# First attention of a two-block transformer kernel: row maxima come out negated, keys carry the factor of an eighth

## The reference, cut to what matters

```
# 8 MoBA heads (one block of 256 keys here, so: causal attention with a bias by distance)
s = q @ k.T * (1 / sqrt(64)) + bias[h, bucket(dist)];  s = where(dist >= 0, s, -inf)
p = softmax(s);  o = p @ v
# 8 sliding-window (SWA) query heads over 2 key heads, window 128, with one learned sink each
s = q @ k.T * (1 / sqrt(64)) + bias[h, bucket(dist)];  s = where(allowed, s, -inf)
m = max(max(s), sink)
p = exp(s - m) / (sum(exp(s - m)) + exp(sink - m));  o = p @ v
# 4 memory heads of width 128 over 256 memory rows
p = softmax(q @ km.T / sqrt(128));  o = p @ vm
```

## Time and profile before

| | |
|---|---|
| median of three runs | 2535.05 us |
| lowest, highest | 2534.59, 2536.48 us |
| span of the profiled execution | 2532.4 us |
| median less span | 2.65 us |
| instructions in the span | 40162 |
| TensorE matmul busy | 2480.0 us, 98% |
| VectorE busy | 1435.8 us, 57% |
| ScalarE busy | 1080.1 us, 43% |
| GpSimd busy | 1313.3 us, 52% |
| first attention, from its first scores to the last unit's output | about 122 to 176 us of the span |

### The profile page before, as it was taken

The page is one execution under the profiler, slowest core; times in us unless marked ns, Lnnn a source line. Parts: engine busy times, 40 slices in busy tenths (PEclk is TensorE's granted clock), DMA queues, the critical chain, the costliest instruction groups (busy, mean ns, idle before and its releaser), DMA issues.

```text
span 2532.4 us, 40162 instructions
## 1 busy us (share of the span) xinstructions
PE 2480.0 (98%) x13612; PEld 2128.2 (84%) x13612; DVE 1435.8 (57%) x3281; ACT 1080.1 (43%) x2021; POOL 1313.3 (52%) x661
## 2 busy tenths in 40 slices
PE   9899999999999999999999999999999999999999
PEld 9789999898888888777888888888888888789888
DVE  5476666379883513565666556665554464755431
ACT  5375555542323332466353222342222343575554
POOL 5628877844434443333434443444443454456887
PEclk9999999999999999999999999999999999999999
DMA  7728545655555432121334444544443453234564
GB/s 243 231 76 256 186 150 185 180 166 189 187 162 146 139 100 76 59 67 51 116 100 145 139 148 135 166 131 149 149 144 110 132 174 123 92 101 150 181 193 141
DMA packets 407170, 365.15 MB, mean 144 GB/s; under 512 B 7564, under 2 KB 398302, under 8 KB 407056
## 3 DMA queue, kind: packets, MB, share of 16 engines
q1 hardware_dynamic: 384840, 339.21, 42.6%
q10 hardware_dynamic: 22216, 24.43, 2.9%
HBM read 362.53 MB, written 1.08 MB: 144 GB/s over the span
## 4 chain that ended last, share of the span: by engine, by line
PE 86%; DVE 5%; POOL 3%; issue 3%; ACT 1%; DMA 1%; SPq 0%; DVEq 0%; POOLq 0%; ACTq 0%
PE bank L2251 67%; PE bank L2261 5%; POOL w_lo L874 3%; PE bank L2259 3%; PE bank L2895 2%; PE bank L2935 1%; PE bank L2349 1%; PE bank L2350 1%; PE bank L2356 1%; ACT w_hi L941 1%; DVE stat L2155 1%; PE bank L2921 1%; PE bank L2497 1%; PE bank L2498 0%; PE bank L2502 0%
## 5 line engine op out<-in xcount | busy, mean ns | idle before, releaser
L874 POOL TENSOR_TENSOR w_lo<-raw,w_hi 128x1024 fp32r<-128x1024 f32 (+3 forms) x557 | 1211.6, 2188 | 1067.3 <-ACT w_hi L941 1067.0
L2251 PE MATMUL bank<-u_both,w_hi 128*128 128x512 f32 (+1 forms) x4240 | 1093.8, 348 | 13.0 <-POOL w_lo L874 6.8
L941 ACT ACTIVATE w_hi<-raw 128x1024 fp32r<-128x1024 f32 (+3 forms) x558 | 534.2, 974 | 1019.7 <-PE bank L2251 817.2
L2251 PEld LDWEIGHTS bank<-u_both,w_hi 128*128 128x128 f32 x4240 | 741.5, 190 | 123.9 <-issue 14.9
L2251 PE MATMUL bank<-u_both,w_lo 128*128 128x512 f32 (+1 forms) x2120 | 734.5, 346 | 0.0
L2251 PEld LDWEIGHTS bank<-u_both,w_lo 128*128 128x128 f32 x2120 | 403.5, 190 | 49.2
L1717 DVE SCALAR_TENSOR_TENSOR bank<-mod_raw,cond,bank 128x256 f32<-128x256 f32 x1008 | 401.2, 482 | 0.4 <-DMA mod_raw<-in_w_mod 0.4
L2251 PE MATMUL bank<-hid_hi,w_hi 128*128 128x512 f32 x528 | 205.7, 390 | 0.0
L2251 PE MATMUL bank<-hid_hi,w_lo 128*128 128x512 f32 x528 | 205.4, 389 | 0.0
L2251 PE MATMUL bank<-hid_lo,w_hi 128*128 128x512 f32 x528 | 205.4, 389 | 0.0
L2039 DVE TENSOR_TENSOR bank<-bank,work 128x512 f32<-128x512 f32 (+1 forms) x88 | 55.5, 630 | 193.8 <-PE bank L2251 186.8
(11 more groups left out here) (327 smaller groups left out, 3617.2 us busy)
## 6 DMA issues: line engine op xcount, KB each, us to landing
mod_raw<-in_w_mod SPq DMA_DIRECT2D x144, 512.0 KB, 4.7
raw<-in_ffn_w_in SPq DMA_DIRECT2D x69, 1024.0 KB, 5.1
raw<-in_w_in SPq DMA_DIRECT2D x67, 1024.0 KB, 5.2
raw<-in_ffn_w_out SPq DMA_DIRECT2D x56, 704.0 KB, 4.7
raw<-in_w_ffn_up SPq DMA_DIRECT2D x22, 1024.0 KB, 5.0
raw<-in_ffn_w_in ACTq DMA_DIRECT2D x19, 1024.0 KB, 5.3
raw<-in_w_attn_out SPq DMA_DIRECT2D x8, 1024.0 KB, 5.1
raw<-in_w_o SPq DMA_DIRECT2D x8, 1024.0 KB, 5.1
```

The lines of the kernel that those rows point to most:

```text
L874: pool.tensor_tensor(st.half(t, w_lo[slot]), st.half(t, block), st.half(t, w_hi[slot]).bitcast(f32), ALU.subtract).then_inc(lo_ready, 1)
L941: act.activation(st.half(t, w_hi[(st.first + c) % 2]), st.half(t, raw_of(st, n)), ACT.Copy).then_inc(hi_ready, 1)
L2251: ins = pe.matmul(dst, s, v, start=first and n == 0, stop=final and n == 2)
```

## The change

Keys of the MoBA and SWA heads are multiplied by 0.125 when they are copied out of PSUM (the copy takes a scale), the bias tables are no longer multiplied by 8, and the exponential's scale is 1 for those units. The reduces for the maxima write negated results (`negate=True`). A MoBA unit then needs no further step: its second reduce raises `nmax_ready`. An SWA unit takes the minimum with the negated sink (a new tile `minus_sinks`, 64 bytes in each partition, filled by one new VectorE instruction). A memory unit still multiplies, now by plus the scale. The two reduces of a MoBA or SWA unit are no longer linked to each other. Behind `minus_sinks` every tile lies 64 bytes further on in SBUF.

```diff
         sinks = sb("sinks", [P, 8])
+        minus_sinks = sb("minus_sinks", [P, 16])
...
-            def copy_tiles(dst, cols):
+            def copy_tiles(dst, cols, scale=1.0):
...
-                                       .rearrange("p (o t) -> p o t", o=1), ACT.Copy).then_inc(taken[b], 1)
+                                       .rearrange("p (o t) -> p o t", o=1), ACT.Copy, scale=scale).then_inc(taken[b], 1)
...
-            gemm("qk_mb", copy_tiles(qk_mb, slice(0, S)))
+            moba_queries, moba_keys = copy_tiles(qk_mb, slice(0, S)), copy_tiles(qk_mb, slice(0, S), 0.125)
+            gemm("qk_mb", lambda st, i, c: (moba_queries, moba_keys)[i](st, i, c))
...
-                        ins = act.activation(k_sw[64 * to:64 * to + 64, kv, :], bank[0][64 * kv:64 * kv + 64, 0:S], ACT.Copy)
+                        ins = act.activation(k_sw[64 * to:64 * to + 64, kv, :], bank[0][64 * kv:64 * kv + 64, 0:S], ACT.Copy, scale=0.125)
...
-                scale = 0.125 if kind != "mem" else 1.0 / math.sqrt(128)
+                scale = 1.0 if kind != "mem" else 1.0 / math.sqrt(128)
...
+            dve.tensor_scalar(minus_sinks[:, 0:8], bank[4][:, 0:8], -1.0, None, ALU.mult)
             dve.tensor_copy(sinks[:, :], bank[4][:, 0:8]).then_inc(taken[4], 1)
...
-                dve.tensor_scalar(tables[:, v, :], bank[5 - v][0:8, :], 8.0, None, ALU.mult).then_inc(taken[5 - v], 1)
+                dve.tensor_copy(tables[:, v, :], bank[5 - v][0:8, :]).then_inc(taken[5 - v], 1)
...
             def max1(n):
                 kind, h = UNITS1[n]
-                scale = 0.125 if kind != "mem" else 1.0 / math.sqrt(128)
                 dve.wait_ge(score_ready, n + 1)
                 st_ = stat[:, n % 2, :]
+                minus = st_[:, 2:4] if kind == "moba" else st_[:, 0:2]
                 if causal(n):
-                    for q in range(2):
-                        link(dve.tensor_reduce(st_[:, q:q + 1], bank[SCORE1[n % 4]][:, q * S:q * S + keys1(n, q)], AX.X, ALU.max))
+                    ins = [dve.tensor_reduce(minus[:, q:q + 1], bank[SCORE1[n % 4]][:, q * S:q * S + keys1(n, q)], AX.X, ALU.max,
+                                             negate=True) for q in range(2)][-1]
                 else:
-                    link(dve.tensor_reduce(st_[:, 0:2], bank[SCORE1[n % 4]][:, :].rearrange("p (q k) -> p q k", q=2), AX.X, ALU.max))
+                    ins = dve.tensor_reduce(minus, bank[SCORE1[n % 4]][:, :].rearrange("p (q k) -> p q k", q=2), AX.X, ALU.max,
+                                            negate=True)
+                if kind == "moba":
+                    ins.then_inc(nmax_ready, 1)
+                    return
+                link(ins)
                 if kind == "swa":
-
-                    link(dve.tensor_scalar(st_[:, 0:2], st_[:, 0:2], scale, sinks[:, h:h + 1], ALU.mult, ALU.max))
-                    dve.tensor_scalar(st_[:, 2:4], st_[:, 0:2], -1.0, None, ALU.mult).then_inc(nmax_ready, 1)
+                    dve.tensor_scalar(st_[:, 2:4], minus, minus_sinks[:, h:h + 1], None, ALU.min).then_inc(nmax_ready, 1)
                 else:
-                    dve.tensor_scalar(st_[:, 2:4], st_[:, 0:2], -scale, None, ALU.mult).then_inc(nmax_ready, 1)
+                    dve.tensor_scalar(st_[:, 2:4], minus, 1.0 / math.sqrt(128), None, ALU.mult).then_inc(nmax_ready, 1)
```

## The result

The changed kernel is slower: 2538.94 us, median of 20 runs (2536.52 to 2541.35), against 2534.45 us for the kernel before over 20 runs (2531.59 to 2537.06). The ratio is 1.0017, with a 95% interval of 1.0011 to 1.0024, so 4.5 us and still within 0.2%. I had forecast 1.0 us less and a range up to 2536.8.

The account below looks back on a forecast made before the run. TensorE holds 86% of the chain, VectorE 5%, leading in the attention from 144.66 to 167.45 us. Gain 0.87 there plus 0.15 at the opening, 1.0 us: 2535.05 becomes 2534.0, range 2530.5 to 2536.8.

Parts of the forecast that it names:

- the 0.15 I counted: Attention's opening: first transpose waits less for unit 0's probabilities, multiplications gone; 0.15 us saved, between 0.1 and 0.27.
- Rival 3: Attention's reduces: linked or not is the same, so 0.8 us gained in all, 2534.3 us; chance 0.14.
- Rival 1: Attention: VectorE drops out of the chain and all TensorE's stalls go, 2.8 us gained, 2532.3 us; chance 0.12.
- Rival 2: Stage behind the attention, led by GpSimd's splits and DMAs: the gain is given back, 2535.05 us; chance 0.10.
- Rival 4: Second block's attention: VectorE's short steps meet GpSimd's splits; one meeting more costs 1.7 us, 2535.8 us; chance 0.09.
- Rival 5: Second block's attention: one meeting less of VectorE's steps with GpSimd's splits on the path, 2532.4 us; chance 0.05.
- What hides the additions: Added negation step, tables' copy, scales and 64-byte shift: each taken as 0 us, the step at most 0.17.

Follow-up runs that it names:

- the last experiment: Changed kernel keeping its 64-byte tile, with 192 bytes more ahead of both blocks' hidden tiles only, against the kernel before: 2531.83 us against 2533.75, ratio 0.9996.

## Why the prediction was wrong

*Its reading of the attention held, step by step.* Two reduces without a link take 0.62 us and not 0.75, 0.13 saved where I took 0.12. From an SWA unit's first reduce to the sum with the sink's term it is 0.79 us, as forecast, against 1.12. Negated output costs nothing: the linked negated pair takes the same 0.75 us. VectorE idles ahead of unit 14's reduce (0.38 us), so TensorE's step of 4.75 us sets the pace. The chain passes to VectorE at 154 us, as forecast, and at the opening the first transpose stands 126.99 − 121.51 = 5.48 us behind the first scores and not 5.63, which is the 0.15 I counted. In total 0.93 us against 1.0. Of the 0.93 the links between the reduces make 0.17, by the run that puts them back.

*Rival 3*, that linking makes no difference, is refuted by 0.93 against 0.79 us in a unit. The rule behind it, in the Trainium skill ("VectorE: DVE Perf Modes", section "The DRAIN you can't avoid"), says that the next step waits for the empty pipe and that leaving semaphores out gains nothing; for these two reduces the measurement says otherwise, and decides. The same section also says that a next instruction that isn't held starts earlier, which fits these two reduces; the prediction left that sentence out. *Rival 1* fell: TensorE still waits for VectorE until 165.71, where the outputs of unit 16 start. Its price was also too high, since the 2.6 us are idle time ahead of weight loads, which run beside products; the products themselves idled 1.79 us from 158 to 168. *Rival 2*, the gain given back behind the attention, is not what made the loss; whether a part of the gain is given back the totals can't tell (their intervals take in 0 as well as 1 us). *Rival 4*, a loss by VectorE's steps meeting GpSimd's splits, had the sign and even named a layout moved by 64 bytes, but not the mechanism; with the hidden tiles put back most of the loss is gone, though the attention's timing is the changed one. *Rival 5* fell with the sign.

*The step that failed* is in "What hides the additions": "The 64-byte shift changes no size or order; with no row that prices it I take 0 and leave it to the range." The runs showed 3.5 us in the products on the hidden tiles and 0.8 in those on `o2` and `m`. The last line of the prediction did name it as a sign of being wrong, "if the layout changes TensorE's pace somewhere", but gave it neither price nor chance. I had counted instructions, and an allocation isn't one. It should have been a part of the change with a price of its own: 1584 products that lie on the chain read a tile that moves. The trace had no row with another distance, so the size could not be read; but the number of products was there, and 2.2 ns each were enough to turn the sign. One nanosecond more or less in each would have been a modest bound, and is 1.6 us; the term had to be in the range and in a rival of its own.

*The accounting.* From the outputs of unit 16 to the end the changed trace loses 4.4 us against the one before (1.7 us ahead at 165.71, 2.7 behind at the end). The layout makes 4.5 of it: 3.5 in the three long pieces, 0.8 between 1240 and 1325 us and 0.2 in the first block's hidden tile. The rest nearly cancels, and comes from things in which executions differ. From the outputs of unit 16 to the first block's down projection, at about 440 us, the changed trace gains 1.3 us. Behind that the granted clock of TensorE matters, which falls to half (1.2 in place of 2.4 GHz) for 3.4 us at a time: once between 1070 and 1100 us in the trace before and not in the changed one, and twice between 2280 and 2350 us in the changed one and not before. Windows as in the earlier trace rows, the clock third from the end, before:

```profile
1070.00:1100.00 30.00, 27.45 (x136) 20.61 (x135) 18.27 (x49) 19.92 (x53) 14.88 (x11) 0.94 0.21 71
2280.00:2350.00 70.00, 64.87 (x531) 63.55 (x530) 39.51 (x94) 39.66 (x69) 47.56 (x22) 1.00 0.47 151
```

After:

```profile
1070.00:1100.00 30.00, 27.45 (x147) 20.61 (x146) 18.71 (x45) 20.96 (x55) 14.73 (x11) 1.00 0.21 71
2280.00:2350.00 70.00, 65.16 (x517) 63.90 (x516) 38.04 (x92) 38.64 (x67) 45.34 (x21) 0.95 0.46 151
```

The first is worth 1.5 us to the changed trace, the second costs it 2.5 by the end. Neither follows the layout: with 256 bytes for the new tile, where the products are the old ones, the trace has the slow clock in both places and loses the same 2.5 us at the second. So two single traces can't be subtracted at their ends; they have to be compared piece by piece. By the pieces the layout's 4.5 less the attention's 0.9 is 3.6 us, and the medians of 20 runs, 4.5 us with an interval of 2.8 to 6.1, agree.

## What to carry to other kernels

A new tile in the middle of the SBUF layout moves all that lie behind it, and products far from the change can get slower by it: pad it to keep the distances of the tiles that TensorE reads (here to 256 bytes), or allocate it last (that was not run). Where only part of the tiles is put back, as in the last experiment, the part of the others stays. A kernel that is one long row of products amplifies a nanosecond; compare the long pieces of the chain, which repeat to 0.02 us here, before looking for a stall. And when an instruction-level sum comes out at 1 us in 2500, the layout belongs in the sum.

## What the runs showed of the hardware

- A 128x512 product (f32 in the profile) took 226.8, 229.0, 232.5 or 233.4 ns from start to start, at a granted clock of 1.00, as the tile that it reads was moved to 0, 64, 128 and 32 or 192 bytes modulo 256 past the weights' tile. The `o2` and `m` tiles gave the same at 0, 64 and 128 bytes (32.64, 32.96, 33.47 us for 144 products).
- Moving both together by 128 bytes changed nothing (119.77 us for 528 products in each), so no address by itself is good or bad. Why the distance matters (weight loads run beside the products, but no run took them away) is open, and for products of another form the best distance was not 0 (63.16 us at 128 bytes, 63.32 at 0, for the stretch on `hid1_both`).
- TensorE's granted clock falls to half for 3.4 or 6.8 us at a time. In ten traces it did so for 6.8 us or more between 2280 and 2350 us, and they lost 2.0 to 2.9 us from there to the end against the trace before, which has no such stretch; a second trace without one (192 bytes) lost nothing.
- A VectorE reduce of PSUM with no wait ahead of it starts before the reduce in front has ended: a pair of 256 and 128 columns took 0.62 us in place of 0.75.
